# Hybrid mixer of a two-network transformer kernel: masks added first, attention in two chains, steps by fixed rank, modulation summed by fours

## The reference, cut to what matters

```
def stick_breaking_attention(q, k, v):
    def block(args):
        q_i, i = args
        z = jnp.einsum('bhqd,bhkd->bhqk', q_i, k) * scale
        qpos = i * SB_BLOCK + jnp.arange(SB_BLOCK)
        mask = kpos[None, :] < qpos[:, None]
        log_fail = jnp.where(mask, jax.nn.log_sigmoid(-z), 0.0)
        later = lax.cumsum(log_fail, axis=3, reverse=True) - log_fail
        a = jnp.where(mask, jnp.exp(jax.nn.log_sigmoid(z) + later), 0.0)
        return jnp.einsum('bhqk,bhkd->bhqd', a, v)

def hybrid_mixer(h, w_in, conv_w, a_log, dt_bias, gdn_norm, sb_q_norm, sb_k_norm, w_out):
    proj = h @ w_in
    gq, gk, gv, gate, ga, gb, sq, sk, sv = _split(proj, HYB_SPLITS)
    qkv = causal_short_conv(jnp.concatenate([gq, gk, gv], axis=-1), conv_w).astype(f32)
    ...
    o_a = gated_delta_rule(qa, ka, va, g, beta)
    o_a = rms_norm(o_a, gdn_norm) * jax.nn.silu(_heads(gate, GDN_HEADS).astype(f32))
    qb = rms_norm(_heads(sq, SB_HEADS).astype(f32), sb_q_norm)
    kb = rms_norm(_heads(sk, SB_HEADS).astype(f32), sb_k_norm)
    o_b = stick_breaking_attention(qb, kb, vb)
    return jnp.concatenate([_merge(o_a), _merge(o_b)], axis=-1).astype(h.dtype) @ w_out
```

## Time and profile before

| | us |
|---|---|
| median of 3 runs | 2945.53 |
| lowest and highest | 2943.82, 2945.81 |
| the profiled execution | 2942.8 |
| its span | 2941.0 |
| PE busy in it | 2805.6 (95%) |
| DVE, ACT, POOL busy | 1423.2, 963.0, 551.5 |
| mean granted TensorE clock | 0.982 |

### The profile page before, as it was taken

One profiled execution on the slowest core, in us unless ns is written; L12 is line 12 of the kernel. 1 busy time (PEld: TensorE's weight loads), 2 busy tenths in 40 slices (PEclk: granted clock), 3 DMA queues, 4 the chain that ended last, 5 costly groups with the idle time before them and its releaser, 6 DMA issues.

```text
span 2941.0 us, 33425 instructions
## 1 busy us (share of the span) xinstructions
PE 2805.6 (95%) x13978; PEld 2257.7 (77%) x13978; DVE 1423.2 (48%) x2090; ACT 963.0 (33%) x1300; POOL 551.5 (19%) x445
## 2 busy tenths in 40 slices
PE   6879989999999999999999999799999998999998
PEld 4757667788888878878888877588888875788886
DVE  5473555667545332354222455555345465444353
ACT  3353444422233222243222343432222344332222
POOL 3455231110122211212101100012112100021121
PEclk9988989999999999999999999899999999999999
DMA  6312203446423222222632322122322321122321
GB/s 238 112 58 68 77 16 127 159 168 226 162 90 110 76 88 74 90 83 90 168 115 83 111 87 68 49 94 84 102 100 82 105 71 66 67 91 79 115 83 68
DMA packets 49799, 294.14 MB, mean 100 GB/s; under 512 B 6346, under 2 KB 6474, under 8 KB 23793
## 3 DMA queue, kind: packets, MB, share of 16 engines
q1 hardware_dynamic: 43632, 274.48, 26.5%
q0 software_dynamic: 4720, 15.20, 2.0%
q10 hardware_dynamic: 1296, 2.32, 0.2%
HBM read 283.33 MB, written 8.65 MB: 99 GB/s over the span
## 4 chain that ended last, share of the span: by engine, by line
PE 87%; DVE 6%; ACT 4%; issue 1%; POOL 1%; DMA 0%; ACTq 0%; DVEq 0%; POOLq 0%
PE ps L218 86%; DVE wlo L211 1%; PE ps L1304 1%; ACT whi L200 0%; DVE F L2232 0%; DMA x<-in_x 0%; ACT F L1321 0%; DVE E L2849 0%; DVE F L412 0%; DVE E L2841 0%; DVE hl L416 0%; DVE E L2844 0%; DVE ada L460 0%; ACT F L1280 0%; DVE F L819 0%
## 5 line engine op out<-in xcount | busy, mean ns | idle before, releaser
L218 PE MATMUL ps<-hh,whi 128*128 128x512 f32 x2088 | 825.0, 395 | 14.1 <-DVE wlo L211 5.2
L218 PE MATMUL ps<-hl,whi 128*128 128x512 f32 x2088 | 814.9, 390 | 0.0
L218 PE MATMUL ps<-hh,wlo 128*128 128x512 f32 x2088 | 814.5, 390 | 0.0
L211 DVE TENSOR_TENSOR wlo<-raw,whi 128x2048 fp32r<-128x2048 f32 (+2 forms) x235 | 493.7, 2101 | 523.6 <-ACT whi L200 523.5
L218 PE MATMUL ps<-R,whi 128*128 128x512 f32 x2080 | 649.7, 391 | 7.8 <-DVE wlo L211 2.8
L200 ACT ACTIVATE whi<-raw 128x2048 fp32r<-128x2048 f32 (+2 forms) x235 | 409.6, 1743 | 688.2 <-PE ps L218 688.2
L218 PEld LDWEIGHTS ps<-hh,whi 128*128 128x128 f32 x2088 | 393.0, 188 | 105.1 <-issue 9.5
L218 PEld LDWEIGHTS ps<-R,whi 128*128 128x128 f32 x2080 | 390.4, 188 | 95.1 <-issue 6.9
L218 PEld LDWEIGHTS ps<-hl,whi 128*128 128x128 f32 x2088 | 393.0, 188 | 83.3
L218 PEld LDWEIGHTS ps<-hh,wlo 128*128 128x128 f32 x2088 | 393.3, 188 | 81.5 <-issue 2.2
L218 PE MATMUL ps<-R,wlo 128*128 128x512 f32 x1040 | 404.7, 389 | 0.0
(11 more groups left out here) (340 smaller groups left out, 2613.6 us busy)
## 6 DMA issues: line engine op xcount, KB each, us to landing
F<-in_ada SPq DMA_DIRECT2D x32, 1024.0 KB, 4.9
raw<-in_fs0in SPq DMA_DIRECT2D x22, 1024.0 KB, 5.9
raw<-in_fs1in SPq DMA_DIRECT2D x22, 1024.0 KB, 4.9
raw<-in_fc0in SPq DMA_DIRECT2D x22, 1024.0 KB, 4.8
raw<-in_fc1in SPq DMA_DIRECT2D x22, 1024.0 KB, 4.8
Rf<-in_ada0h SPq DMA_DIRECT2D x24, 512.0 KB, 3.5
raw<-in_fs0out SPq DMA_DIRECT2D x16, 704.0 KB, 4.9
raw<-in_fs1out SPq DMA_DIRECT2D x16, 704.0 KB, 4.3
```

The source lines that it names most:

```text
L211: e.tensor_tensor(m.wlo[n % 2][:, 0:size], m.raw[m.slot[n]][:, 0:size], m.whi[n % 2][:, 0:size].bitcast(F32), SUB).then_inc(*s.up("wlo", n))
L218: return e.matmul(out, l, r, start=start, stop=stop, skip_group_check=True)
```

## The change

Five things are altered.
- Masks: a new constant `stickmask` (0, or -1e30 where a key is not before the query) is loaded once, and DVE makes z straight from the scores, times 1/8 plus mask, in four pieces. ACT then makes |z|, exp of its negative and ln; DVE's max/add follows; `smask`, `negs`, POOL's part and ACT's copies go.
- Attention is two chains: `stick` (values, the pairs' slabs, norms) and `heads` (the eight heads). A pair's slab may run while heads of the pair before are under way. The norm's sums move from bank 5 to bank 6.
- `hybrid_order` takes the chain whose next step can start first; only between equal starts a fixed rank decides, with `stick` last. Steps can `need` others' ends (`gates`, `pair`, `scores`, `values`, `inverse`, `modulation`), and their times are waited for.
- The table's durations are changed, and 0.2 instead of 0.15 is put between steps.
- Modulation: four tiles to a group (`ADA_BATCH`), one wait of PE and one DVE instruction of 4 columns for each group. The number of tiles and DMAs stays.

```
-H_LM, H_SM, H_U, H_V, H_Q, H_K = 3072, 3968, 4224, 7808, 9856, 10368
+H_LM, H_MK, H_SM, H_U, H_V, H_Q, H_K = 3072, 3520, 4032, 4288, 7872, 9920, 10432
...
-def step(work, mark=None, beside=""):
+def step(work, mark=None, beside="", needs=(), done=None):
...
 def head_steps(h):
-    yield step("pe:1.8", ("needs", "gates"))
+    yield step("pe:1.8", needs=("gates",))
...
+    for work in ("dve:1.4", "pe:1.8", "dve:2"):
         yield step(work)
-    yield step("pe:0.5", None, "dve:1.4 pool:0.8")
+    yield step("pe:0.5", None, "dve:1.4 pool:1")
...
         yield step("pe:0.5", None, "pool:0.8")
-        for work in ("act:0.4", "pe:0.7", "dve:0.6"):
+        for work in ("act:0.4", "pe:1", "dve:0.6"):
...
-    yield step("act:0.6", None, "pool:1.3")
+    yield step("act:0.6", None, "pool:1.5", needs=("modulation",) if h == 2 else ())
...
-        yield step("pe:2.9 act:0.4", ("free",))
+        yield step("pe:2.9 act:0.4", ("free",), done=("values", j))
...
-        yield step("act:2.4", ("free",))
-        for work in ("pe:0.9", "act:1.4", "pe:0.9", "act:1.4", "dve:0.7"):
+        yield step("act:2.6", ("free",), needs=(("scores", 2 * p - 1),) if p else ())
+        for i in range(2):
+            yield step("pe:0.9 act:0.7", ("six", "sb_rs_ln", p, i))
+            yield step("act:0.7")
+        yield step("dve:1.6", done=("pair", p))
+
+
+def stick_head_steps():
+    for h in range(8):
+        yield step("pe:1.5 dve:1.3", ("six", "sb_z", h, 1), needs=(("pair", h // 2),))
+        yield step("pe:0.7 dve:0.7", ("six", "sb_z", h, 3), done=("scores", h))
+        for work in ("act:3.9", "dve:1.7", "pe:2.2"):
             yield step(work)
-        for h in (2 * p, 2 * p + 1):
-            yield step("pe:1.5 act:1", ("six", "sb_z", h, 1))
-            yield step("pe:0.7 act:0.6", ("six", "sb_z", h, 3))
-            for work in ("dve:1.5", "act:2.6", "dve:1.5"):
-                yield step(work)
-            yield step("dve:0.9", None, "pool:1.5")
-            yield step("pe:2.2")
-            yield step("pe:1.3", ("six", "sb_sub", h, 1), "dve:1.3")
-            yield step("pe:0.7")
-            yield step("pe:0.3 dve:0.7", ("six", "sb_sub", h, 3))
-            yield step("act:1.3")
-            yield step("pe:2.2")
-            yield step("act:0.6", ("needs", "inverse", 3) if p == 3 else None)
-            yield step("dve:0.7")
+        yield step("pe:1.3", ("six", "sb_sub", h, 1), "dve:1.3")
+        yield step("pe:0.7")
+        yield step("pe:0.3 dve:0.7", ("six", "sb_sub", h, 3))
+        yield step("act:1.3")
+        yield step("pe:2.2", needs=(("values", 1),))
+        yield step("act:0.6", needs=(("inverse", 3),) if h >= 6 else ())
+        yield step("dve:0.7")
+
...
+ADA_BATCH = 4
...
 def ada_steps():
-    for j in range(16, 40, 2):
-        yield step("pool:4.9 dma:3.4")
-        yield step("pool:4.9")
-        yield step("pe:0.3 dve:0.2 dma:3.1", ("six", "mod", "h", j + 1))
+    for j in range(16, 40, ADA_BATCH):
+        for _ in range(ADA_BATCH):
+            yield step("pool:5.4 dma:3.4")
+        yield step("pe:0.5 dve:0.2", ("six", "mod", "h", j + ADA_BATCH - 1), done="modulation" if j + ADA_BATCH == 40 else None)
...
+FIRST_CHOICE = ("gates", "heads", "delta0", "delta1", "ada", "stick")
+BEGIN = {"gates": 1.0, "ada": 13.0, "heads": 1.0, "delta1": 20.0, "delta0": 0.0, "stick": 1.0}
...
-    order, slabs, before, held, last, done = [], [], {}, False, None, set()
-
-    def able(i):
-        if at[i] == len(chains[i]):
-            return False
-        mark = chains[i][at[i]][1] or ("",)
-        return not (held and mark[0] == "slab") and (mark[0] != "needs" or mark[1:] in done)
-
-    while any(n < len(c) for n, c in zip(at, chains)):
-        start = {i: max(ready[i], free[chains[i][at[i]][0][0][0]]) for i in range(5) if able(i)}
-        soon = min(start.values()) + 0.7
-        i = max((i for i in start if start[i] <= soon), key=lambda i: left[i])
...
+    while any(at[i] < len(chains[i]) for i in chains):
+        start = {}
+        for i in FIRST_CHOICE:
+            if at[i] < len(chains[i]):
+                work, mark, _, needs, _ = chains[i][at[i]]
+                if all(n in when for n in needs) and not (held and mark and mark[0] == "slab"):
+                    start[i] = max([ready[i], free[work[0][0]]] + [when[n] for n in needs])
+        i = min(start, key=start.get)
...
+            now += 0.2
+        if done:
+            when[done] = now
...
+        e.dma_start(m.f(H_MK), m.dram["stickmask"]).then_inc(*s.dma("stickmask"))
...
             s.wait_ge("sb_sq", p, i)
-            if i:
-                s.wait_ge("sb_rs_ln", p, 0)
-            elif p:
-                s.wait_ge("sb_lo", 2 * p - 1)
-            mm(e, m.ps[5][:, :], m.k("bones"), m.tmp[i]).then_inc(*s.up("sb_sum", p, i))
+            six_free(s, "sb_rs_ln", p, i)
+            mm(e, m.ps[6][:, :], m.k("bones"), m.tmp[i]).then_inc(*s.up("sb_sum", p, i))
             yield from steps(2)
         yield
+
+
+def pe_stick_heads(e, s, m):
+    v = stick_values(m)
+    for p in range(4):
         for hh in range(2):
             h, rows = 2 * p + hh, slice(64 * hh, 64 * hh + 64)
             q, k = m.f(H_Q)[rows, :], m.f(H_K)[rows, :]
-            if hh == 0:
-                s.wait_ge("sb_q", p, 1)
-                s.wait_ge("sb_rs_ln", p, 1)
+            s.wait_ge("sb_q", p, 1)
...
+def act_stick_heads(e, s, m):
+    for p in range(4):
         for hh in range(2):
             h, rows = 2 * p + hh, slice(64 * hh, 64 * hh + 64)
+            yield from steps(2)
+            s.wait_ge("sb_z", h, 3)
             if h:
-                s.wait_ge("sb_pv", h - 1)
-            for c in range(4):
-                s.wait_ge("sb_score", h, c)
-                e.activation(stick_z(m, c), m.ps[5 + c % 2][:, 0:T - c * P], ACT.Copy, scale=0.125).then_inc(*s.up("sb_z", h, c))
-                if c % 2:
-                    yield
-            yield
-            s.wait_ge("sb_sp", h, 0)
-            e.activation(stick_sp(m), stick_sp(m), table(e, s, ACT.Exp)).then_inc(*s.up("sb_exp", h, 0))
+                s.wait_ge("sb_cum", h - 1, 3)
+            e.activation(stick_sp(m), stick_z(m), ACT.Abs).then_inc(*s.up("sb_exp", h, 0))
             s.wait_ge("sb_exp", h, 0)
-            e.activation(stick_sp(m), stick_sp(m), table(e, s, ACT.Ln), bias=m.eps[:, 1:2]).then_inc(*s.up("sb_exp", h, 1))
-            yield from steps(7)
+            e.activation(stick_sp(m), stick_sp(m), table(e, s, ACT.Exp), scale=-1.0).then_inc(*s.up("sb_exp", h, 1))
...
+            s.wait_ge("stickmask")
+            if h:
+                s.wait_ge("sb_pv", h - 1)
+            for c in range(4):
+                s.wait_ge("sb_score", h, c)
+                w = T - c * P
+                e.scalar_tensor_tensor(out=stick_z(m, c), in0=m.ps[5 + c % 2][:, 0:w], scalar=0.125, in1=m.f(H_MK, w), op0=MUL, op1=ADD).then_inc(*s.up("sb_z", h, c))
...
+            yield
+            s.wait_ge("sb_exp", h, 2)
+            e.scalar_tensor_tensor(out=sp, in0=z, scalar=0.0, in1=sp, op0=MAX, op1=ADD).then_inc(*s.up("sb_sp", h))
...
-            s.wait_ge("sb_z", h, 3)
-            if h:
-                s.wait_ge("sb_cum", h - 1, 3)
-            e.scalar_tensor_tensor(out=sp, in0=z, scalar=-1.0, in1=z, op0=MUL, op1=MIN).then_inc(*s.up("sb_sp", h, 0))
-            yield from steps(2)
-            s.wait_ge("sb_exp", h, 1)
-            e.scalar_tensor_tensor(out=sp, in0=z, scalar=0.0, in1=sp, op0=MAX, op1=ADD).then_inc(*s.up("sb_sp", h, 1))
-            yield
-            s.wait_ge("sb_sp", h, 1)
-            for c in range(4):
-                a = stick_sp(m, c)[:, 0:P]
-                t = e.tensor_tensor(a, a, m.k("smask"), MUL)
-            t.then_inc(*s.up("sb_mask", h))
-            yield from steps(2)
-            s.wait_ge("sb_negs", h)
             for c in range(4):
...
 def pe_ada_chain(e, s, m):
-    for j in range(16, 40, 2):
-        yield from steps(2)
-        six_free(s, "mod", "h", j + 1)
-        s.wait_ge("ada_h", "h", j, 7)
-        pe_ada(e, s, m, j // 2 % 2, 2, 6, ("h", j + 1), "ada_h")
+    for j in range(16, 40, ADA_BATCH):
+        last = j + ADA_BATCH - 1
+        yield from steps(ADA_BATCH)
+        six_free(s, "mod", "h", last)
+        s.wait_ge("ada_h", "h", last, 7)
+        for c in range(ADA_BATCH):
+            t = mm(e, m.ps[6][:, c:c + 1], ada_sum(m, c), m.k("ones")[:, 0:1])
+        t.then_inc(*s.up("ada_sum", "h", last))
...
-        s.wait_ge("ada_sum", *(("h", (j - 4) // 2 * 2 + 1) if j >= 20 else ("first", 3)))
+        s.wait_ge("ada_sum", *(("h", j // ADA_BATCH * ADA_BATCH - 1) if j >= 20 else ("first", 3)))
...
-        if j % 2:
+        if (j + 1) % ADA_BATCH == 0:
             yield
...
 def act_hybrid(e, s, m):
-    merged(act_gdn(e, s, m, 0), act_gdn(e, s, m, 1), act_stick(e, s, m), steps(36), act_gdn_gates(e, s, m))
+    merged(delta0=act_gdn(e, s, m, 0), delta1=act_gdn(e, s, m, 1), stick=act_stick(e, s, m),
```

(4 more changed lines are left out.)

133 lines of the change are left out of this document (68 added, 65 removed).

## The result

The changed kernel takes 2933.39 us (median of 6 executions, 2931.86 to 2936.73) against 2944.96 of before: ratio 0.9963, 95% interval 0.9952 to 0.9973. That is 11 us faster where 38 were forecast. The time lies at the edge of the stated range (2880 to 2934) and outside the forecast's own (2892 to 2920); the direction is right, the size is a third of the forecast.

The account below looks back on a forecast made before the run. PE's order and waits, no full engine, bound the hybrid stage. Work 333 plus loss 28 ahead of and 25 in the tail gives 386 against 424 us, 38 less: 2907 us; own range 2892 to 2920, stated range 2880 to 2934.

Parts of the forecast that it names:

- the cut: Stage split at 378 us, where its last dense slab ends: 66 us of loss ahead of it, 25 behind.
- the tail: Behind the last dense slab: 60 us of work and 25 of loss, as at present; loss bounds 5 and 55.
- The rival of a slower tail: Chains behind the last dense slab take turns, 115 us there; total 2971; chance 0.08.
- Masks first: Attention heads: mask work moved or dropped saves 2.0 us a head; 10 of 21.8 us of PE waits go.
- z on DVE: Attention scores: PE's third score piece waits for the first z, now made by DVE; cost taken as 2 us.
- 28 instead of 66: Stage ahead of the last dense slab: loss falls from 66 us to 28 (banks 6, clock 8, late steps 12, z 2).
- Banks, forecast 6: Where a slab directly follows another, PE waits 0.69 us for a bank's emptying, about nine places: 6 us.
- Late steps 12 and z 2: Ahead of the tail: 12 us for steps late where DVE is dense with convolutions, 2 for z on DVE.
- Counting uncovered hops: Dependent hops too little covered on PE, by the programs' step tables: 26 before, 8 after, ahead of the last 60 us.
- Modulation at nothing: Modulation by fours on POOL: last tile near 288 us, before PE needs it; priced at nothing, up to 20 if DMAs lag.
- The idle only moves: Rival: steps placed by fixed durations come late elsewhere, stage loss stays 91 us; total 2945; chance 0.08.
- POOL paces the middle: Rival: PE waits in order for sums of four modulation tiles, losing 20 us of the gain; 2927; chance 0.14.

Follow-up runs that it names:

- copyfirst: Changed kernel with one step moved: ACT's copy of the third queries-and-keys slab out of banks 0 and 1 precedes a head's abs, exp and ln; ratio 0.9941.
- bank: Changed kernel with one planner line more: a slab can't be planned before banks 0 and 1 are emptied; 2927.37 us, ratio 0.9928.
- coarse: Changed kernel with dense pieces of 12 matmuls instead of 6, all but the stage's first slab; 2948.39 us, ratio 1.0009.
- masks: Kernel before with the mask part alone (mask constant, z on DVE, absolute value on ACT), old list kept; 2950.77 us, ratio 1.0013.
- masksplan: The kernel masks, old structure and rule, with the table adapted to the new mask work and the list planned anew; 2938.80 us, ratio 0.9980.
- oldpick: Changed kernel with the earlier rule for choosing chains (start within 0.7 us of the earliest, most work left); 2926.31 us, ratio 0.9931.
- bankold: The kernel bank with oldpick's rule for choosing among chains; 2942.84 us, ratio 0.9997.
- early: The kernel bank with seven eighths of the output projection's first slab moved into PE's last two waits of the stage; 2919.51 us, ratio 0.9917.
- earlyada: The kernel early plus modulation steps counted 0.46 us later by the planner and both delta chains begun at 0; 2919.52 us, ratio 0.9910.

## Why the prediction was wrong

**What bounds the stage, the cut, the tail: right.** PE's order and waits bound it, no engine became full, and the tail took 86.6 us where 60 of work and 25 of loss were forecast. The trace has 12.8 us of idle in it and 12 for the clock (PE is busy for 24 us at 1.2 GHz). That the tail doesn't gain because one delta head is alone with attention heads in series fits this, but no run separates it. The rival of a slower tail, from 100 us upward, did not come.

**Masks first: right in its prices, right in size only in company.** 2.0 us a head were forecast, 1.7 measured in the new list; the waits for the mask went. But alone, in the old list, the part gave nothing. The sum could not see this, since it added parts that were each priced in the trace of before. The Trainium skill, page "ScalarE: Activation LUTs", section "Rules for kernel authors", puts max, min, add and multiply on VectorE; read as a rule against the move, it would have made |z| on ACT a loss. ACT took 1270 ns and DVE 1608 for the same fp32 elements, so here the measurement speaks against it; the page gives its reason for bf16, which no run here has.

**z on DVE: right, and cheaper than taken.** PE waited 0.2 us for L2861 in all; 2 were taken.

**"28 instead of 66" for the middle: the step that failed.** Measured, 330.3 - 273 = 57. By its terms:
- *Banks, forecast 6 (nine places at 0.69).* 18.4. I took the length of this wait from the old list and did not ask what stands ahead of the copy on ACT in the new one. The diff shows `held = False` at the choosing of the step, and `needs` with their times beside it. This alone would have named slab gdn 6. copyfirst prices that one wait at some 6 us, bank prices all of them with the new list at 10.
- *Half clock, forecast 8.* Of the 54 us at 1.2 GHz in the stage 27 lie ahead of the tail, and PE is busy in 22 of them: 11.
- *Late steps 12 and z 2.* The other visible idle of the middle is 330.3 - 300.9 - 18.4 = 11. Right.
- *Nothing was forecast for what the trace counts as busy.* What is left is 57 - 18 - 11 - 11 = 17 us, the largest miss beside the banks. The prediction knew this loss (pipelines that run out before a dependent step) and put no term of it into the 28: for the list of before the same sum is 66 - (333.0 - 296.1) - 34.7/2 = 12.

So 12 of the 17 us were there before, and the new list adds 5. In the list of before 22 dense pieces start behind small groups, in the new one 59, and the first matmul of such a piece holds up its next: 0.335 us in the middle one of 57 of these places, against 0.229 inside a slab. The same is seen where a slab starts after a wait, from 354.69 to this one:

```profile
355.02 0.40 PE L218 MATMUL ps<-hh,wlo 128*128 128x512 f32 x1
```

That makes 37 x 0.1 = 4 us. Behind 64x64 groups the piece also starts 0.149 us after the last small matmul, where it is 0.031 behind 128x128 ones; there are 19 such places now and one before, another 2. Over the whole stage PE's busy time at one clock (as in coarse) rose by 7 us, from 345 to 352, so the two nearly make it up. The other lists agree: it is 342 to 348 us in the six with 22 to 35 such places (before, masks, masksplan, coarse, oldpick, bankold) and 349 to 353 in the eight with 45 to 61. This is a relation over fourteen lists and not an experiment that changes nothing else.

**Counting uncovered hops: a wrong measure.** My count of 26 against 8 used the same table as the planner, and a list chosen by that table looks good in it. The table plans 404 us for the old list and 373 for the new one, 31 less; the chip gives 7. oldpick is planned at 408 and takes 405, bank at 389 and takes 402, coarse at 403 and takes 432. What the table didn't enforce, the banks' emptying, was a part of the new list's planned gain: enforcing it lengthens the plan by 16 us and shortens the run by 10.

**Modulation at nothing: the waits right, the price wrong.** Its DMA waits on POOL fell to 77.3 us and PE waited for no sum, as forecast, though the last sum came at 314 us, 26 later than worked out: POOL also stood 19.3 us for PE's sums ahead of L2927, a wait that I had not in the sum. But batches of four give another list than twos, and the two differ by 16 us, 10 with the banks' emptying in the plan.

**The rivals.** "The idle only moves", 2945 at 0.08, was nearest in mechanism: the mask's waits went and the copies' waits came. Its time was 12 us off. "POOL paces the middle" came nearer in time, 2927, but by luck: PE waited for no sum.

## What to carry to other kernels

Where a planner with a table of durations writes the order, look first for what it doesn't enforce: compare, step by step, planned starts with the planned ends of what the hardware will wait for, and set the largest misfits beside the waits in a trace. Don't judge a new order by the table while the plan leaves such a wait out, and don't add up edits that each redraw the list: here the lists ranged over 25 us and two good edits cancelled each other. Local edits to one list were easier to forecast (copyfirst, early and earlyada all fell inside their ranges): find the bare wait at the end of a stage and move into it work of the next stage that is ready.

## What the runs showed of the hardware

The granted clock matters beside the idle that one sees. Kernels with the same matmuls spent between 37 and 96 us of this stage at 1.2 GHz, and masks lost in clock what it gained in idle: busy time 385.69 against 371.75 at 8 us less idle. Matmuls whose result nobody reads raised the tail's clock from 0.84 to 0.93. A dense piece of six matmuls between small groups costs about 0.1 us more than six inside a slab, and 0.12 more again behind groups on 64x64 blocks.
